# A two-block model on one core: the recurrence's first unit placed in the last input tile, and the key search of the expert stage spread differently

## The chip, the cores and the metric

One core of a Trainium2 chip runs the whole program in one launch. The metric is the device time of one execution in microseconds (us), the median of the runs taken. In the text TensorE is PE, VectorE is DVE, ScalarE is ACT, GpSimd is POOL and SyncE is SP, as in the profile's rows.

## The reference

256 tokens of width 2048 go through three layers, all in float32:

```python
def even_layer(x, ...):            # layer 1
    proj = rmsnorm(x, ln) @ w_in   # 2048 -> A: q, k, v, gate; B: q, f, i, gate
    ya = sliding_window_attention(...) * silu(ag)
    logf = logaddexp(log(max(lb, 1e-30)), log1p(-lb) + log_sigmoid(bf))
    ob = hgrn2_chunkwise(silu(bq), logf, -expm1(logf), bi)   # gated recurrence, 8 heads of 128
    yb = rmsnorm(ob, gn) * silu(bg)
    return x + concat([ya, yb]) @ w_out
def odd_layer(x, ...):             # layer 2: stick-breaking attention, 16 heads
    return x + (oc * silu(cg)) @ w_out
# layer 3: SSD and forgetting attention side by side, w_out, and then an expert layer
def peer(h, wq, k1, k2, u, v):
    q = (t @ wq).reshape(T, 8, 2, 128)
    v1, i1 = top_k(q[:, :, 0] . k1, 16);  v2, i2 = top_k(q[:, :, 1] . k2, 16)
    sc, pos = top_k(v1[..., :, None] + v2[..., None, :], 16)   # 16 of 256 pairs
    idx = 128 * i1 + i2 at pos;  g = softmax(sc)
    act = gelu(sum(u[idx] * t));  return sum(g * act * v[idx])  # 128 rows of u and of v per token
# and a last rmsnorm
```

The expert layer gathers 256 x 128 rows of 8 KB from `u` and as many from `v`.

## The kernel before, in words

**Projections.** Seven matrix products (even_in, even_out, odd_in, odd_out, two_in, two_out, peer_q) run in 57 tiles of 512 output columns. SP loads a tile's weights in four quarters into RAW. Each tile is split in eight subs: ScalarE rounds a sub of the weights to WH (`split`, L613), VectorE writes what the rounding left to WL (L1110), TensorE multiplies (HH, HL: the high and low part of the activations) with both (L1741). WH and WL hold four subs, so ScalarE can be at most four subs ahead of TensorE. Sub `s` of tile `t` is called place `8t + s`; every engine has a function `beside(place)` that puts work of other stages in front of a sub. The order of each engine's queue is thus written out by hand. A tile's result is taken out of its PSUM banks by `leave`, at sub 4 of the next tile or at the end of a phase. For a `silu` tile VectorE scales the result to BIG, and ScalarE applies silu to it (L565).

**The even layer.** Tiles 0 to 12 are even_in, 13 to 16 even_out. The gates of the recurrence are ready from place 91 on. TensorE turns the first log decays at place `B_TURN` = 101, ScalarE copies them to LFT at place 103. When even_in is over and its last tile has left, the recurrence runs over 16 units (8 heads x 2 halves of the tokens): `log_decays` (PE, ACT), `decays_low` (DVE), `level_sums` (PE, L2033 on), `decays` (ACT: Exp, L908), `query` (DVE, L1535), the key product (POOL, L472) `products` (PE), `masked` (DVE, L1547 on), `values` (PE), then per head a square sum and a norm (`normed`), and `y_high`, `y_low` put the result into HH and HL. The attention's eight outputs lie in BIG 3 and 4 and go to HH and HL in one operation each (`y_high_eight`, `y_low_eight`), before unit 1 overwrites them. Then tile 13 begins: ScalarE, VectorE and TensorE in turn.

**The expert stage.** Tiles 53 to 56 are peer_q. The key scores of a query tile are multiplied beside the next tile, the last ones behind tile 56. The key search of the first 128 tokens is cut in 4 pairs of heads with 8 steps each (`top_part`: steps 0 to 3 take the top 16 of 128, 4 and 5 the top 16 of 256 pairs, 6 and 7 the indices). It starts at place 439, one step a place: 17 steps fit. Then VectorE does 7 more, computes the normed tokens TT (L1696), and enters the loop over 256 picks (128 for each half of the tokens): one dot of 128x2048 with a gathered U row (L1701), the last 8 steps beside the first 8 dots, a small product every 4 picks for the coefficients; ScalarE then makes diagonals (L1036), and TensorE multiplies them with V rows. POOL issues all gathers (L533 and L542): U row n waits for dot n - 6 (six buffers), V row n - 8 follows it, and waits for TensorE's row n - 14. UROW lies on RAW and WL, so the first issue waits for the last split of tile 56, and the fifth for its last matmul. The second half's search goes beside picks 12 to 105, its step every third.

## Time and profile before

| what | value |
|---|---|
| median of 3 runs | 2936.0 us (2935.48 to 2937.61) |
| profiled execution | 2937.92 us, span 2936.2 us |
| granted TensorE clock, mean | 0.976 |
| busy in the span | PE 2467.8 us, DVE 1629.0, ACT 948.7, POOL 698.7 |
| DMA | 779.65 MB, of it 537.15 MB by POOL's queue (the gathered rows) |

Times in rows count from the span's start. A timeline row has start, duration, engine, line, operation, and in brackets how long the engine stood idle before it and what released it. A clock of 1.00 is 2.4 GHz, 0.50 is 1.2 GHz. The busy time of TensorE is modelled from pipelined matmuls, so it is no measure of use.

### The profile page before, as it was taken

The numbers are of one execution on the slowest core, as the hardware profiler recorded it, in microseconds if no ns is written. First come the engines' busy times: TensorE is split into PE (matmuls) and PEld (weight loads), VectorE is DVE, ScalarE is ACT, GpSimd is POOL, SyncE is SP. The second block draws the span as 40 slices with busy tenths as digits, with TensorE's granted clock in tenths as the row PEclk, the third lists the DMA queues.
The fourth block names the chain that finished last, engine by engine and source line by source line (L and its number), as shares of the span: only waits on it lengthen the run. The fifth ranks groups of instructions, "written<-read, shape, count | busy, mean of one in ns | idle before, by whom it ended". The sixth has DMA issues, their size and how long they took to land.

```text
span 2936.2 us, 30854 instructions
## 1 busy us (share of the span) xinstructions
PE 2467.8 (84%) x12244; PEld 1757.5 (60%) x12244; DVE 1629.0 (55%) x2253; ACT 948.7 (32%) x1548; POOL 698.7 (24%) x751
## 2 busy tenths in 40 slices
PE   7999888999999899999899287777777777777776
PEld 6997777899889789888689132222222322222222
DVE  4757495544455554456457966656555445444444
ACT  4557454533676444444554010000010001000001
POOL 5003151000000000540000243333333333333331
PEclk9999999999999999999899699999999999999999
DMA  5643304555444446333354799999999999999997
GB/s 190 212 147 129 129 1 144 172 186 179 153 157 158 158 135 215 129 115 116 101 191 139 315 406 421 421 422 421 422 421 422 421 422 422 421 422 422 421 422 319
DMA packets 200415, 779.65 MB, mean 266 GB/s; under 512 B 16564, under 2 KB 20880, under 8 KB 134096
## 3 DMA queue, kind: packets, MB, share of 16 engines
q0 software_dynamic: 74400, 537.15, 44.2%
q1 hardware_dynamic: 125872, 240.53, 24.7%
q8 instruction: 97, 1.59, 0.2%
q14 instruction: 46, 0.38, 0.0%
HBM read 775.54 MB, written 2.10 MB: 265 GB/s over the span
## 4 chain that ended last, share of the span: by engine, by line
DMA 34%; PE 26%; DVE 5%; issue 1%; ACT 1%; POOL 0%; DVEq 0%; ACTq 0%; POOLq 0%
DMA VROW<-in_peer_v_dram,WORK 34%; PE bank L1741 25%; DMA UROW<-in_peer_u_dram,WORK 1%; DVE WL L1110 1%; DVE BIG L1701 1%; DVE WORK L1406 0%; DVE BIG L1407 0%; DVE WORK L1409 0%; DVE WORK L1408 0%; PE bank L1800 0%; DVE WORK L1405 0%; ACT WH L613 0%; DVE BIG L1416 0%; DVE WORK L1418 0%; DVE BIG L1414 0%
## 5 line engine op out<-in xcount | busy, mean ns | idle before, releaser
L1741 PE MATMUL bank<-VROW,WORK 128*128 128x512 f32 x2024 | 928.5, 604 | 366.6 <-DMA VROW<-in_peer_v_dram,WORK 299.7
L1741 PEld LDWEIGHTS bank<-VROW,WORK 128*128 128x128 f32 x2024 | 368.4, 191 | 926.1 <-issue 744.6
L1701 DVE CUSTOM_DVE_ANT_0 BIG<-UROW,bank 128x2048 f32<-128x2048 f32 x256 | 585.5, 2288 | 562.6 <-DMA UROW<-in_peer_u_dram,WORK 548.0
L1110 DVE TENSOR_TENSOR WL<-RAW,WH 128x1024 fp32r<-128x1024 f32 (+2 forms) x456 | 543.0, 1200 | 528.7 <-ACT WH L613 527.3
L1741 PE MATMUL bank<-HH,WH 128*128 128x256 f32 x2128 | 609.1, 286 | 8.4 <-issue 4.8
L613 ACT ACTIVATE WH<-RAW 128x1024 fp32r<-128x1024 f32 (+2 forms) x456 | 464.2, 1034 | 445.1 <-PE bank L1741 444.7
L1741 PE MATMUL bank<-HL,WH 128*128 128x256 f32 x2128 | 603.3, 284 | 0.0
L1741 PE MATMUL bank<-HH,WL 128*128 128x256 f32 x2128 | 603.2, 283 | 0.0
L1741 PEld LDWEIGHTS bank<-HH,WH 128*128 128x128 f32 x2128 | 407.7, 192 | 15.9 <-issue 14.0
L1741 PEld LDWEIGHTS bank<-HL,WH 128*128 128x128 f32 x2128 | 407.8, 192 | 0.1
L1741 PEld LDWEIGHTS bank<-HH,WL 128*128 128x128 f32 x2128 | 407.7, 192 | 0.0
L542 POOL DMA_INDIRECT VROW<-in_peer_v_dram,WORK x256 | 241.7, 944 | 686.7 <-PE bank L1741 668.0
L533 POOL DMA_INDIRECT UROW<-in_peer_u_dram,WORK x256 | 243.7, 952 | 315.4 <-DVE WL L1110 195.1
L1741 PE MATMUL bank<-WH,HH 128*128 128x512 f32 (+1 forms) x736 | 291.4, 396 | 29.2 <-DVE WL L1110 29.2
L1045 ACT ACTIVATE WORK<-WORK 128x4 f32<-128x4 f32 x64 | 13.1, 205 | 920.1 <-DVE WORK L1701 920.1
L1741 PE MATMUL bank<-WH,HL 128*128 128x512 f32 (+1 forms) x736 | 287.1, 390 | 0.0
L1741 PE MATMUL bank<-WL,HH 128*128 128x512 f32 (+1 forms) x736 | 286.8, 390 | 0.0
L500 POOL TENSOR_SCALAR WORK<-GT,SM 128x128 f32<-128x128 f32 x16 | 19.5, 1219 | 713.9 <-DVE SM L1496 674.4
L1741 PEld LDWEIGHTS bank<-WH,HH 128*128 128x128 f32 x736 | 140.7, 191 | 60.4 <-issue 32.4
L1741 PEld LDWEIGHTS bank<-WL,HH 128*128 128x128 f32 x736 | 140.5, 191 | 28.8
L1741 PEld LDWEIGHTS bank<-WH,HL 128*128 128x128 f32 x736 | 140.8, 191 | 27.1
L1036 ACT ACTIVATE WORK<-ID,WORK 128x128 f32<-128x128 f32 x253 | 87.6, 390 | 211.9 <-PE bank L1741 206.2
(325 smaller groups left out, 1729.7 us busy)
## 6 DMA issues: line engine op xcount, KB each, us to landing
RAW<-in_w_in_odd_dram SPq DMA_DIRECT2D x64, 1024.0 KB, 5.1
RAW<-in_w_in_even_dram SPq DMA_DIRECT2D x48, 1024.0 KB, 5.0
RAW<-in_w_in_dram SPq DMA_DIRECT2D x44, 1024.0 KB, 4.9
RAW<-in_w_out_even_dram SPq DMA_DIRECT2D x16, 1024.0 KB, 5.0
RAW<-in_w_out_odd_dram SPq DMA_DIRECT2D x16, 1024.0 KB, 5.0
RAW<-in_w_out_dram SPq DMA_DIRECT2D x16, 1024.0 KB, 5.3
RAW<-in_peer_wq_dram SPq DMA_DIRECT2D x16, 1024.0 KB, 5.2
UROW<-in_peer_u_dram,WORK POOLq DMA_INDIRECT x256, 27.0
```

Source lines behind the costliest of these rows:

```text
L500: pool.tensor_scalar(g[:, 0:P], GT[:, :], lf[:, 0, h:h + 1], None, ALU.mult)
L533: pool.indirect_dma_start(UROW[:, n % ROWS_EACH, :], None, a["peer_u_2"], bass.IndirectOffsetOnAxis(ap=PICK[:, m, pick:pick + 1], axis=0))\
L542: pool.indirect_dma_start(VROW[:, v % ROWS_EACH, :], None, a["peer_v_2"], bass.IndirectOffsetOnAxis(ap=PICK[:, m, pick:pick + 1], axis=0))\
L613: act.activation(WH[:, sl:sl + 2, 0:w], raw[:, k0:k0 + 2, 0:w], ACT.Copy)\
L1036: act.activation(DIAG[:, k % 4, :], ID[:, :], ACT.Copy, scale=COEF[:, n:n + 1])\
L1045: act.activation(GELU[:, cols], DOT[:, cols], ACT.Gelu).then_inc(s["p_gelu"], 1)
L1110: dve.tensor_tensor(WL[:, sl:sl + 2, 0:w], raw[:, k0:k0 + 2, 0:w], WH[:, sl:sl + 2, 0:w].bitcast(F32), ALU.subtract).then_inc(s["wl_done"], 1)
L1701: dve.tensor_tensor_reduce(out=JUNK[:, n % 2, :], in0=UROW[:, b, :], in1=TT, op0=ALU.mult, op1=ALU.add, scale=1.0, scalar=0.0, accum_out=D ...
L1741: return pe.matmul(dst, lhsT, rhs, start=start, stop=stop, skip_group_check=True)
```

## The change

Two seams are changed.

In the even layer the transposes of the first two units' log decays move to places 95 and 98, their copies and low parts to 96 to 100, and `level_sums(0)` to place 101, in banks 2 and 3. `decays(0)`, `query(0)` and `products(0)` come before the last tile leaves; that tile's silu comes behind `decays(1)`. The attention's outputs go to HH and HL in two halves. LFL1 moves to another place in SBUF (onto RDIAG), so that unit 1's low part no longer overwrites them. Four subs of tile 13 are rounded and split within the recurrence, at iterations 6, 8, 10 and 12, and left out in the tile itself.

In the expert stage only pair 0 is searched inside tiles 54 to 56, one step every second place. Pairs 1 to 3 go beside picks 4 to 27, gates are made per pair, and the second half's search beside picks 29 to 91, a step every second. U rows 0 to 3 wait only for the splits whose RAW quarter they overwrite. The dots begin when half of the scores are out.

```diff
-TOP_AT, TOP_EVERY = 12, 3
+TOP_AT, TOP_EVERY = 29, 2
+TOP_INSIDE = TOP_STEPS
-B_TURN = 101
+B_TURN = 95
+B_LOW, B_TURN_1, B_LOW_1, B_LEVELS = 97, 98, 100, 101
...
# POOL
+                if u == 1:
+                    pool.wait_ge(s["y_l"], 8)
...
-                    if n == 0:
-                        pool.wait_ge(s["wl_done"], 8 * N_TILES)
+                    if n < 4:
+                        pool.wait_ge(s["wl_done"], 8 * (N_TILES - 1) + 2 * (n + 1))
...
# ScalarE
+                    if t == OUT_TILE and sub < 4:
+                        continue
...
+            def split_ahead(sub):
+                t = OUT_TILE
+                if sub % 2 == 0:
+                    act.wait_ge(s[f"w_full{sub // 2}"], 16 * (t + 1))
+                act.wait_ge(s["ws_used"], 8 * t + (sub - 3))
+                raw = RAW[:, sub // 2, :].rearrange("p (k n) -> p k n", k=4)
+                k0 = 2 * (sub % 2)
+                act.activation(WH[:, 2 * sub:2 * sub + 2, :], raw[:, k0:k0 + 2, :], ACT.Copy).then_inc(s["wh_done"], 1)
...
+            def y_high_four(kt, tile):
+                act.wait_ge(s["y_ready"], 8)
+                act.wait_ge(s["ws_used"], 8 * OUT_TILE)
+                act.activation(HH[:, kt:kt + 4, :], tile.rearrange("p (b t) -> p b t", t=T), ACT.Copy)\
+                    .then_inc(s["y_h"], 4)
...
-                if place == B_TURN + 2:
+                if place == B_TURN + 1:
                     log_decays(0)
+                if place == B_TURN_1 + 1:
+                    log_decays(1)
...
-                    act.wait_ge(s["y_l"], 8)
+                    act.wait_ge(s["y_l"], 4)
...
-            log_decays(1)
             decays(0)
-            y_high_eight(0, 0, BIG[:, 3:5, :])
+            y_high_four(0, BIG[:, 3, :])
+            y_high_four(4, BIG[:, 4, :])
...
+                if i == 0:
+                    leave(*pending.pop())
+                if i in (6, 8, 10, 12):
+                    split_ahead((i - 6) // 2)
...
+                if q in (3, 5, 7):
+                    gate_exp(0, (q - 1) // 2, 1)
...
# VectorE
+                if place == B_LOW:
+                    decays_low(0)
+                if place == B_LOW_1:
+                    decays_low(1)
-                step = step_at(place, TOP_FIRST, 1, TOP_STEPS * 4)
+                step = step_at(place, TOP_FIRST, 2, TOP_INSIDE)
...
-            decays_low(0)
-            y_low_eight(0, 0, BIG[:, 3:5, :])
-            decays_low(1)
             query(0)
+            leave(*pending.pop())
+            y_low_four(0, BIG[:, 3, :])
+            y_low_four(4, BIG[:, 4, :])
+            masked(0)
...
+                if i in (6, 8, 10, 12):
+                    split_ahead((i - 6) // 2)
...
-            inside = 8 * (Q_TILE + 4) - TOP_FIRST
-            for step in range(inside, 3 * TOP_STEPS):
-                top_part(0, step // TOP_STEPS, step % TOP_STEPS)
             dve.wait_ge(s["ln_in"], 16)
-            dve.wait_ge(s["q_s"], 8)
+            dve.wait_ge(s["q_s"], 4)
...
+                if n == 2:
+                    dve.wait_ge(s["q_s"], 8)
...
-                if n < TOP_STEPS:
-                    top_part(0, 3, n)
-                if n == TOP_STEPS:
-                    gates(0)
+                step = step_at(n, BATCH, 1, 3 * TOP_STEPS)
+                if step is not None:
+                    top_part(0, 1 + step // TOP_STEPS, step % TOP_STEPS)
+                if n == 4:
+                    gates(0, 0, 1)
+                i = step_at(n, 16, 10, 3)
+                if i is not None:
+                    gates(0, 1 + i, 1)
...
# TensorE
+                if place == B_TURN_1:
+                    log_decays(1)
+                if place == B_LEVELS:
+                    pe.wait_ge(s["tile_free"], OUT_TILE - 1)
+                    level_sums(0)
...
-            log_decays(1)
-            level_sums(0)
+            products(0)
+            pe.wait_ge(s["t_scaled"], sum(r["n"] for r in RUNS if r["phase"] == "even_in" and r["kind"] == "silu"))
```

## Rows read from the trace of the kernel before

**Rows 1.** Page, section 2: 40 slices of 73.4 us, what DMA moved.

```profile
GB/s 190 212 147 129 129 1 144 172 186 179 153 157 158 158 135 215 129 115 116 101 191 139 315 406 421 421 422 421 422 421 422 421 422 422 421 422 422 421 422 319
```

**Rows 2.** Page, section 4: the chain that ended last, shares by engine.

```profile
DMA 34%; PE 26%; DVE 5%; issue 1%; ACT 1%; POOL 0%; DVEq 0%; ACTq 0%; POOLq 0%
```

**Rows 3.** Windows: length, busy us (count) by engine, PEclk, DMA share, GB/s.

```profile
1605.00:1620.00 15.00, 14.72 (x123) 14.52 (x122) 14.24 (x35) 4.33 (x5) 0.00 (x0) 1.00 0.00 1
1620.00:1640.00 20.00, 7.02 (x57) 6.60 (x56) 18.62 (x60) 2.46 (x4) 6.11 (x6) 0.79 0.78 297
1620.00:1700.00 80.00, 25.14 (x95) 14.64 (x95) 76.36 (x172) 7.65 (x18) 27.92 (x29) 0.66 0.86 336
1750.00:2850.00 1100.00, 808.01 (x1758) 318.59 (x1759) 575.17 (x717) 92.22 (x291) 414.97 (x440) 0.99 1.01 422
```

**Rows 4.** Timeline of POOL, gathers of the expert stage.

```profile
1622.69 1.09 POOL L533 DMA_INDIRECT UROW<-in_peer_u_dram,WORK  x1 [195.15 <-DVE WL L1110]
...
1687.90 0.94 POOL L542 DMA_INDIRECT VROW<-in_peer_v_dram,WORK  x1 [6.26 <-PE bank L1741]
```

**Rows 5.** Timeline of DVE, from tile 56 to the first dots.

```profile
1585.94 1.23 DVE L1110 TENSOR_TENSOR WL<-RAW,WH 128x1024 fp32r<-128x1024 f32 x1
1589.57 1.22 DVE L1110 TENSOR_TENSOR WL<-RAW,WH 128x1024 fp32r<-128x1024 f32 x1
...
1620.58 1.23 DVE L1110 TENSOR_TENSOR WL<-RAW,WH 128x1024 fp32r<-128x1024 f32 x1
...
1639.03 2.36 DVE L1696 SCALAR_TENSOR_TENSOR bank<-XR,SM,BIG 128x2048 f32<-128x2048 f32 x1
...
1678.13 2.29 DVE L1701 CUSTOM_DVE_ANT_0 BIG<-UROW,bank 128x2048 f32<-128x2048 f32 x1
```

**Rows 6.** Timeline of ACT, roundings and score evictions of tile 56.

```profile
1602.53 1.06 ACT L613 ACTIVATE WH<-RAW 128x1024 fp32r<-128x1024 f32 x1 [0.91 <-PE bank L1741]
...
1612.88 1.06 ACT L613 ACTIVATE WH<-RAW 128x1024 fp32r<-128x1024 f32 x1 [1.76 <-PE bank L1741]
...
1628.32 0.69 ACT L801 ACTIVATE BIG<-bank,SM 128x512 f32<-128x512 f32 x1 [0.21 <-PE bank L1741]
```

**Rows 7.** Timeline of DVE, last eviction of even_in, mask of unit 1.

```profile
355.30 1.29 DVE L1081 TENSOR_TENSOR BIG<-bank,RS 128x512 f32<-128x512 f32 x2 [6.22 <-PE bank L1741]
...
375.48 0.68 DVE L1547 TENSOR_TENSOR WORK<-bank,BIG 128x512 f32<-128x512 f32 x1
```

**Rows 8.** Timeline of ACT, places 96 on and the first decays.

```profile
321.23 1.06 ACT L613 ACTIVATE WH<-RAW 128x1024 fp32r<-128x1024 f32 x1 [2.49 <-PE bank L1741]
...
358.39 1.28 ACT L908 ACT_TABLE_LOAD   x1
359.69 0.60 ACT L908 ACTIVATE WORK<-bank 128x512 f32<-128x512 f32 x1
```

**Rows 9.** Timeline of PE, the last attention values, at place 96.

```profile
331.01 0.86 PE L1741 MATMUL bank<-BIG 128*64 128x256 f32 x4
```

**Rows 10.** Windows inside the recurrence and at its end.

```profile
430.00:440.00 10.00, 8.24 (x62) 7.17 (x60) 9.78 (x14) 6.29 (x13) 5.87 (x3) 1.00 0.00 0
450.00:455.00 5.00, 1.23 (x7) 0.64 (x6) 1.34 (x3) 3.93 (x7) 0.00 (x0) 0.88 0.00 0
```

**Rows 11.** Timelines of DVE and POOL, one y_low and one key product.

```profile
435.05 2.30 DVE L1163 TENSOR_TENSOR HL<-YB,HH 128x256 fp32r<-128x256 f32 x1
...
434.93 2.13 POOL L472 TENSOR_TENSOR WORK<-WORK,BIG 128x896 f32<-128x896 f32 x1 [0.35 <-ACT WORK L908]
```

**Rows 12.** Timeline of PE, end of the recurrence, first matmul of tile 13.

```profile
452.84 0.70 PE L1741 MATMUL bank<-BIG,ONES 128*128 128x256 f32 x2 [2.31 <-ACT BIG L915]
...
460.08 0.77 PE L1741 MATMUL bank<-WH,HH 128*128 128x512 f32 x1 [6.54 <-DVE WL L1110]
```

**Rows 13.** Timeline of ACT, fifth rounding of tile 13.

```profile
465.02 1.06 ACT L613 ACTIVATE WH<-RAW 128x1024 fp32r<-128x1024 f32 x1 [3.50 <-PE bank L1741]
```

**Rows 14.** Page, section 5: the V row matmuls.

```profile
L1741 PE MATMUL bank<-VROW,WORK 128*128 128x512 f32 x2024 | 928.5, 604 | 366.6 <-DMA VROW<-in_peer_v_dram,WORK 299.7
```

More of the change, by code:

```diff
@@ L123 @@
 ODD_TILE = last_tile("even_out") + 1
+OUT_TILE = first_tile("even_out")
 C_FIRST = 8 * ODD_TILE + 70
@@ L907, in decays @@
                 for b in range(2):
-                    ins = act.activation(B_EX[u % 2][:, 512 * b:512 * (b + 1)], bank[b][:, :], ACT.Exp)
+                    ins = act.activation(B_EX[u % 2][:, 512 * b:512 * (b + 1)], bank[b if u else 2 + b][:, :], ACT.Exp)
                 ins.then_inc(s["b_ex"], 1)
@@ L1008, in _, with gate_exp @@
             scores_out(3)
-            def gate_exp(m):
-                act.wait_ge(s["tk_e"], 4 * (m + 1))
-                act.activation(GATE[:, m * PICKS:(m + 1) * PICKS], GATE[:, m * PICKS:(m + 1) * PICKS], ACT.Exp)\
-                    .then_inc(s["tk_g"], 1)
+            def gate_exp(m, i, pairs):
+                act.wait_ge(s["tk_e"], 4 * m + i + pairs)
+                cols = GATE[:, m * PICKS + 32 * i:m * PICKS + 32 * (i + pairs)]
+                act.activation(cols, cols, ACT.Exp).then_inc(s["tk_g"], pairs)
             def square(b):
@@ L1105, in split @@
                             leave(*pending.pop())
+                    if t == OUT_TILE and sub < 4:
+                        continue
                     dve.wait_ge(s["wh_done"], 8 * t + sub + 1)
@@ L1113, in split, with split_ahead @@
                     pending.append((r, i, parity, t))
+            def split_ahead(sub):
+                dve.wait_ge(s["wh_done"], 8 * OUT_TILE + sub + 1)
+                raw = RAW[:, sub // 2, :].rearrange("p (k n) -> p k n", k=4)
+                k0 = 2 * (sub % 2)
+                dve.tensor_tensor(WL[:, 2 * sub:2 * sub + 2, :], raw[:, k0:k0 + 2, :],
+                                  WH[:, 2 * sub:2 * sub + 2, :].bitcast(F32), ALU.subtract).then_inc(s["wl_done"], 1)
             def phase(name):
                 over_tiles(dve, name, split)
-                if not name.endswith("out"):
+                if not name.endswith("out") and name != "even_in":
                     leave(*pending.pop())
@@ L1164, in y_low, with y_low_four @@
                                   ALU.subtract).then_inc(s["y_l"], 1)
+            def y_low_four(kt, tile):
+                dve.wait_ge(s["y_h"], kt + 4)
+                dve.tensor_tensor(HL[:, kt:kt + 4, :], tile.rearrange("p (b t) -> p b t", t=T),
+                                  HH[:, kt:kt + 4, :].bitcast(F32), ALU.subtract).then_inc(s["y_l"], 4)
             def y_low_eight(c, kt, tiles):
@@ L1459, in beside @@
                         dve.wait_ge(s["tk_iota"], 1)
-                    top_part(0, step // TOP_STEPS, step % TOP_STEPS)
+                    top_part(0, 0, step)
                 for n in range(1, 4):
@@ L1652, in _, with gates @@
             phase("peer_q")
[L1653 to L1659 removed]
+            def gates(m, i, pairs):
+                dve.wait_ge(s["tk_g"], 4 * m + i + pairs)
+                g3 = GATE[:, m * PICKS + 32 * i:m * PICKS + 32 * (i + pairs)].rearrange("p (h k) -> p h k", k=16)
+                gs = gsum[:, 0:2 * pairs]
+                link(dve.tensor_reduce(gs, g3, AX.X, ALU.add))
+                link(dve.reciprocal(gs, gs))
+                link(dve.tensor_tensor(g3, g3, gs.unsqueeze(2).broadcast_to([P, 2 * pairs, 16]), ALU.mult))
             def coefficients(q):
@@ L1710, in _ @@
                 if n == GATES_AT:
-                    gates(1)
-                if n == TOP_STEPS:
-                    coefficients(0)
-                if n > TOP_STEPS and n % BATCH == 1:
+                    gates(1, 0, 4)
+                if n > BATCH and n % BATCH == 1:
                     coefficients(n // BATCH - 1)
@@ L1805, in phase @@
                 over_tiles(pe, name, tile)
-                if not name.endswith("out"):
+                if not name.endswith("out") and name != "even_in":
                     pe.wait_ge(s["tile_free"], last_tile(name) + 1)
@@ L1933, in log_decays, with level_sums @@
                     .then_inc(s["b_lt"], 1)
+            def level_sums(u):
+                m = u % 2
+                if u == 0:
+                    pe.wait_ge(s["b_ms"], 4)
+                pe.wait_ge(s["b_ll"], u + 1)
+                if u >= 1:
+                    pe.wait_ge(s["b_ex"], u)
+                if m == 0:
+                    ends = MSR[:, 512:1024]
+                else:
+                    ends = MSR[:, 512:1536 - 256].rearrange("p (a b) -> p a b", b=256)[:, 0:3:2, :]
+                first = bank[0] if u else bank[2]
+                mm(first, LFT[:, m, :], MSR[:, 0:512], True, False)
+                mm(first, LFL[m], MSR[:, 0:512], False, True)
+                dst = bank[1].rearrange("p (a b) -> p a b", b=256) if m else bank[1] if u else bank[3]
+                mm(dst, LFT[:, m, :], ends, True, False)
+                mm(dst, LFL[m], ends, False, True).then_inc(s["b_es"], 1)
             keys = KEYS.rearrange("p (f d) -> p f d", f=16)
```

55 lines of the change are left out of this document (16 added, 39 removed).

## The prediction

> **What bounds the kernel now.** I read the slices of the page first [rows 1]: up to some 1600 us DMA moves 1 to 215 GB/s, then from slice 25 on 421 to 422 in all but the last. The chain that ended last says the same [rows 2]: projections on TensorE, then expert rows by DMA. So each half has its own currency: before the expert stage a microsecond counts if TensorE's order of work gets shorter; in it, if DMA starts earlier or idles less. The change touches one seam in each half, and the windows and timelines around the two seams give the rest.
>
> **Seam B, the start of the expert stage.** From 1605 to 1620 us DMA moves 1 GB/s [rows 3]. The first U row is issued at 1622.69 [rows 4], right behind the last split of the input tile (1620.58, 1.23 us) [rows 5]. From 1620 to 1700 us the queues move 336 GB/s, in the steady stretch 422 [rows 3]: 80 x 336 / 422 = 63.7 us of work in 80, so 16.3 us lost. Why is in the timeline of VectorE [rows 5]: after the last split VectorE does the rest of pair 2 and the expansion TT (1639.03), so the first dot starts at its end, 1641.4. Six row buffers fill, then wait for a dot at every step of the key search that is woven in. The ninth dot starts at 1678.13; eight picks with eight steps take 36.7 us, 4.59 each.
>
> One pick is two row sets of 1.049 MB, 2.485 us each at 422 GB/s, 4.97 together. New order, in the times of the profile of before:
> - VectorE puts 8 steps on places 439 to 453 instead of 17 on 439 to 455. The split of place 452 waits for ScalarE's rounding (1602.53 + 1.06) [rows 6], and so ends near 1604.8. Step 7 takes 3.63 - 1.15 = 2.5 us (the distance of two splits less one split) [rows 5]: the indices of pair 0 are ready at 1607.4. U rows 0 to 2 follow at about 1607.5 to 1610. Row 3 follows the last split, which no longer queues behind steps: rounding at 1612.88 [rows 6] + 1.06 + 1.23 = 1615.2.
> - Those four rows (9.9 us of transfer) run where DMA idles today. TT then runs from 1615.2 to 1617.6, dots 0 and 1 to 1622.3. Dot 2 waits for the last scores, which are evicted from 1628.32 on [rows 6]: 1628.2 to 1630.6.
> - Row 4 waits for the last matmul of the tile, about 1624.2, and is issued near 1625.0 (before, the issue followed the split's end by 0.9 us). Before, the first issue at 1622.69 was worth full rate from 1625.9: 1640 less 20 x 297 / 422 = 14.1 us for what had moved [rows 3]. That is 3.2 us after the issue; I take 2.9, as TensorE ends the tile 0.3 us sooner without the late splits. Full rate from 1627.9.
> - Rows 4 to 7 keep DMA busy until 1637.8, and the reload of LNF 2.5 us more. Row 8 is free to go at 1630.7, so there is no gap. From dot 4 on VectorE needs 4.59 us for a pick with a step, and I put 0.14 on it for coefficient products and the smaller gates (three or four instructions of 0.2 to 0.3 us in eight picks): 4.73 against 4.97 of DMA. It stays ahead by little, and the backlog at dot 8 is some 15 us.
> - V rows no longer start with ScalarE and TensorE far behind. Before, V row 6 is issued at 1687.90, after 6.26 us of waiting for TensorE [rows 4]. Now diagonal 0 is made after dot 7 (1649), and v_used 1 comes near 1655.5, before POOL needs it with dot 8's row.
>
> Sum: the old stream is worth a start at 1620 + 16.3 = 1636.3 for 512 row sets; the new one 1627.9 for 508, that is 1627.9 - 9.9 = 1618.0. Gain 18.3 us. Bounds: 13 if VectorE loses 5 us in the first 24 picks, 20 if the ramp is shorter. The search of the second 128 tokens only moves its 32 steps within the loop (29 to 91 instead of 12 to 105); a dot is 2.3 of the 4.59, a step the other 2.3, so a pair of picks there costs 6.9 us under 9.9: nothing. The waits on wl_done and the smaller exponentials cost nothing for the same reason.
>
> **Seam A, the recurrence.** Removed in front: before, TensorE ends the even input tile at 355.1 (VectorE's eviction at 355.30 is released by it) [rows 7], ScalarE does silu and an Exp table load and makes the first decays at 359.69 [rows 8], and the mask of unit 1 starts at 375.48 [rows 7]. After, the first unit's decays, query and key products are made inside the tile. What this adds there:
> - ScalarE at place 96 now waits for a transpose that TensorE issues at place 95. Before, ScalarE rounds place 96 at 321.23 [rows 8] while TensorE is at place 92; place 96 begins at 331.0 [rows 9]. So ScalarE's queue stands 7 us, and its four places of lead shrink to one; rounding 1.06 and split 1.23 just fit into a place of 2.82 (1.06 busy and 1.76 waiting at 1612.88) [rows 6]. At place 99 the same once more: it waits for place 98, which begins at 331.2 + 0.86 + 2 x 2.82 = 337.7. Behind it stands the eviction of tile 11 at place 100: VectorE ends split 99 at 340.6, the low part and the eviction at 342.2, silu at 343.3, rounding 344.3, split 345.6. TensorE wants it at 337.7 + 0.2 + 2 x 2.82 = 343.6: a stall of 2.0 us. With the two transposes and four matmuls of level_sums (0.93 us, work moved and not new) the tile ends at 357.9, not 355.1. Bounds: 0.9 to 5 us.
> - After it, with the durations of before (a half of HH 1.0 us, a half of HL 1.2, a mask 2.1): products(0) at once, HH and HL until 362.0, mask 0 until 364.1, decays of unit 1 at 361.3, silu with its table load until 364.8, Exp load and decays of unit 2 until 367.6. Query 2 and the key product of unit 2 then start together, and mask 1 starts between 368.9 and 370.5. Against 375.48 this is 5.0 to 6.6 us earlier; I take 6.0.
>
> Added in the loop: four roundings on ScalarE (1.06 each, hidden: it is busy 6.29 of 10 us there) and four splits on VectorE. VectorE is busy 9.78 of 10 us there [rows 10], so nothing hides them: 4 x 1.2 = 4.8 us. From both sides: 0, if each falls into the wait that y_low has now, and 9.6, if each also meets a GpSimd operation. The row for this: the y_low of 128x256 takes 2.30 us at 435.05 and ends at 437.35, as the key product on GpSimd (434.93 to 437.06) does [rows 11]. A split in front of it takes over that wait and adds its own 1.2 behind, so I stay at 4.8. By the Trainium skill (SBUF — State Buffer, Who interferes with whom), a VectorE instruction with two SBUF inputs and a GpSimd instruction that reads SBUF lock one another out for a whole instruction, by issue order. The trace agrees with 2.30 us against 1.23 for a tile four times as wide. By that rule a split that issues first could hold back the next 0.6 us GpSimd product as well; with 0.6 x 4 the price would be 7.2.
>
> Removed behind: TensorE's last work of the loop is at 452.84 and ends at 453.5; its next matmul waits for the split until 460.08 [rows 12]. The four first splits are done by then, so TensorE goes on at 453.5. Before, the first eighth of the tile ends at 465.0 (ScalarE's rounding at 465.02 is released by it) [rows 13]. After, it ends at 453.5 + 2.7 = 456.2 at full clock. The later eighths are rounded from 457.7 on, and TensorE wants the fifth at 464.4: no new wait. Gain 8.7 us. The clock is a risk: it is 0.88 over 450 to 455 [rows 10], the full level until about 453.8 and then 1.2 GHz. Were it to fall with TensorE at work, up to 2 us are lost.
>
> By the Trainium skill (ScalarE: Activation LUTs, What ACT_TABLE_LOAD costs) a change of table set costs about 2.66 us with its drain. The trace does not agree: a load of 1.28 at 358.39 is followed by the exponential at 359.69 [rows 8]. By the page's price the two loads around the moved silu would take 2.8 us more from seam A.
>
> Seam A: 6.0 - 4.8 + 8.7 = 9.9 us. Everything between the seams is paced by TensorE and moves as a whole.
>
> **Total.** 18.3 + 9.9 = 28.2 us. The profiled execution has a span of 2936.2 and took 2937.9; it becomes 2908.0 and 2909.7. The median, 2936.0, is 1.9 us below the profiled run: 2907.8.
>
> **Rivals.**
> - B only: seam A gives nothing. The places at 96 to 100 cost 5 instead of 2.8, each loop split meets a lock (9.6), and the clock falls at the tail (2): 9.9 - 2.2 - 4.8 - 2 = 0.9. Then 2936.0 - 19.2 = 2916.8. For it: VectorE is full; against: all three have to come.
> - VectorE becomes the bound of the first 24 picks: a pick with a step needs 5.4 instead of 4.73, 0.43 over DMA's 4.97, so 24 x 0.43 = 10 us, and 2918. Against: the 4.59 are measured with DMA at full rate.
> - Slower: TensorE stays at 1.2 GHz in the expert stage. Today it wakes on six V rows that lie ready. After, it gets four diagonals at a time and may stand between. The mean clock over 1620 to 1700 is 0.66 [rows 3]. A V row takes 928.5 / 253 = 3.67 us at full clock [rows 14], 7.3 at half, 2.4 more than DMA needs for a pick. From 12 such picks on (28 / 2.4) the gain is gone; with 40, 2936 - 28 + 96 = 3004. Against: the steady stretch keeps 0.99 with TensorE busy 808 of 1100 us, so idle 1.3 in every pick [rows 3].
> - The U rows before the tile's end don't overlap (the indices come too late): 9.9 us less, 2917.7.
>
> **Chances.** Forecast 0.72, B only 0.12, VectorE bound 0.05, early rows lost 0.05, slower 0.03; 0.03 for a gain that is larger, as no stall at place 100 and free splits give 2900. 0.2% of this kernel, 5.9 us, is about what a measurement can tell from no change. Range 2898 to 2920: down by the 6.8 of the cheap ends of seam A and 2 of the ramp, up to the cases that lose one seam. Faster 0.95, same 0.02, slower 0.03.
>
> **What would show it.** Three or four U issues before the last matmul of the last query tile and DMA busy there; the first dot near 1617 less the shift of seam A; no window under 400 GB/s from 10 us after; TensorE's first output-tile matmul within 1 us of the last square sum; y_low or split of 2.3 us or more in the loop; a gap of some 2 us at place 100. Wrong would be: dots 5 to 27 spaced over 4.97 on average, PEclk at 0.5 behind dot 20, or a loop longer by over 7 us.

## The result and the profile after

The median went from 2936.8 us (four runs, 2935.5 to 2937.6) to 2916.6 us (four runs, 2916.3 to 2917.2), a ratio of 0.9931 with a 95% interval of 0.9916 to 0.9945. In another group of runs, on other executions of both kernels, it came out at 2916.8 and 0.9932 [0.9918, 0.9945]. The forecast was 2907.8, range 2898 to 2920. So the sign and the range held, and 8.1 us of the gain are missing: 20.1 instead of 28.2.

The two seams are read one by one. First the DMA rate in the 40 slices of the page after, the row that answers to [rows 1]:

```profile
GB/s 191 210 152 130 130 15 130 173 188 179 155 155 163 159 135 206 128 116 131 89 186 160 368 421 421 421 421 421 422 422 421 413 422 422 422 421 422 421 422 313
```

The steady rate starts in the 24th slice, before in the 25th, and the 23rd has 368 instead of 315. One slice of 72.9 us has 413 for 421; before has no such slice. The windows that answer to [rows 3] (same columns):

```profile
1605.00:1620.00 15.00, 14.88 (x125) 14.68 (x123) 9.31 (x7) 2.20 (x3) 4.53 (x3) 1.00 0.76 277
1620.00:1640.00 20.00, 2.02 (x16) 1.86 (x16) 16.14 (x36) 3.99 (x7) 12.12 (x13) 0.67 0.91 362
1620.00:1700.00 80.00, 49.42 (x111) 21.44 (x112) 73.67 (x166) 10.90 (x25) 36.77 (x38) 0.83 0.99 407
1750.00:2850.00 1100.00, 812.71 (x1757) 319.56 (x1755) 584.36 (x751) 92.24 (x291) 416.39 (x440) 0.99 1.01 421
```

Where DMA moved 1 GB/s it moves 277, the 80 us behind it have 407 instead of 336, and the steady stretch is as before. The timelines of GpSimd (gathers) and VectorE (dots) after, which answer to [rows 4, 5]:

```profile
1603.14 1.10 POOL L539 DMA_INDIRECT UROW<-in_peer_u_dram,WORK  x1 [180.19 <-DVE WORK L1505]
...
1610.99 2.80 POOL L539 DMA_INDIRECT UROW<-in_peer_u_dram,WORK  x1 [3.96 <-DVE WL L1149]
1620.16 0.94 POOL L539 DMA_INDIRECT UROW<-in_peer_u_dram,WORK  x1 [6.36 <-PE bank L1804]
```
```profile
1613.03 2.29 DVE L1762 CUSTOM_DVE_ANT_0 BIG<-UROW,bank 128x2048 f32<-128x2048 f32 x1
...
1623.31 2.29 DVE L1762 CUSTOM_DVE_ANT_0 BIG<-UROW,bank 128x2048 f32<-128x2048 f32 x1 [5.54 <-PE bank L1804]
...
1636.59 2.29 DVE L1762 CUSTOM_DVE_ANT_0 BIG<-UROW,bank 128x2048 f32<-128x2048 f32 x1
...
1640.63 2.29 DVE L1762 CUSTOM_DVE_ANT_0 BIG<-UROW,bank 128x2048 f32<-128x2048 f32 x1
...
1644.68 2.29 DVE L1762 CUSTOM_DVE_ANT_0 BIG<-UROW,bank 128x2048 f32<-128x2048 f32 x1
```

The first dot is at 1613.03 instead of 1641.4. These three dots with a short search step between them are 4.05 us apart (1636.59, 1640.63, 1644.68). The steps are not alike: over dots 5 to 27 the mean distance is 4.71 us and the longest 6.32. The mean is under the 4.97 that DMA needs for a pick.

Seam A lost its lead on the way. VectorE after: the last eviction of the input tile and the mask of unit 1, which answer to [rows 7].

```profile
357.50 1.29 DVE L1117 TENSOR_TENSOR BIG<-bank,RS 128x512 f32<-128x512 f32 x2 [6.35 <-PE bank L1804]
...
368.83 0.69 DVE L1604 TENSOR_TENSOR WORK<-bank,BIG 128x512 f32<-128x512 f32 x1
```

The mask is 6.65 us earlier than in before, and the first norm 6.6. (A norm's time is here the start of its last VectorE instruction, the subtraction of 128x256.) Then come four pairs of steps with a split. One of them, VectorE and under it GpSimd after (answers to [rows 11]):

```profile
404.20 1.92 DVE L1617 TENSOR_TENSOR YB<-YB,BIG 128x256 f32<-128x256 f32 x1
...
409.29 3.10 DVE L1159 TENSOR_TENSOR WL<-RAW,WH 128x1024 fp32r<-128x1024 f32 x1
```
```profile
403.75 2.09 POOL L478 TENSOR_TENSOR BIG<-BIG 128x896 f32<-128x896 f32 x1 [3.51 <-ACT BIG L936]
...
408.84 2.47 POOL L478 TENSOR_TENSOR WORK<-WORK,BIG 128x896 f32<-128x896 f32 x1 [3.00 <-ACT WORK L936]
```

The split starts 0.45 us behind a key product of GpSimd and takes 3.10 us instead of the 1.23 that it takes elsewhere. In the same pair a two-input subtraction of 128x256, 0.42 us elsewhere, starts 0.45 us behind the other key product and takes 1.92. A pair took 10.54 us before; with a split the distances of the norms are 11.66, 12.48, 12.35 and 12.37, together 6.7 us more. TensorE at the end of the recurrence after, which answers to [rows 12]:

```profile
445.68 3.48 PE L1804 MATMUL bank<-BIG 128*128 128x128 f32 x16 [2.15 <-DVE AMB L1605]
...
455.13 0.70 PE L1804 MATMUL bank<-BIG,ONES 128*128 128x256 f32 x2 [2.49 <-ACT BIG L943]
455.48 0.58 PE L1804 MATMUL bank<-WH,HH 128*128 128x512 f32 x1
```

The next projection does start right behind the last square sum, without a wait, but at 455.48 and not at 453.5, and with TensorE's clock at the lower level twice on the way. Windows of after (columns as in [rows 10]):

```profile
445.00:450.00 5.00, 4.32 (x22) 4.30 (x23) 2.37 (x5) 0.39 (x2) 0.00 (x0) 0.66 0.01 3
450.00:455.00 5.00, 2.26 (x18) 1.87 (x17) 2.24 (x5) 3.95 (x6) 0.00 (x0) 1.00 0.00 0
455.00:460.00 5.00, 4.87 (x14) 3.91 (x15) 1.18 (x3) 3.93 (x6) 0.00 (x0) 0.66 0.00 0
```

ScalarE's fifth rounding of the tile, which answers to [rows 13]:

```profile
460.26 1.06 ACT L622 ACTIVATE WH<-RAW 128x1024 fp32r<-128x1024 f32 x1 [0.24 <-PE bank L1804]
```

460.26 instead of 465.02: 4.8 us of seam A are left.

### The profile page after: what moved, and what is told of

Same layout as the page of the kernel before. It is cut to its first block, busy times and chain, and to the rows that moved or that the text cites. A ratio compares the mean times of both kernels' runs of the same rounds, so it can differ in the third digit from the quotient of the medians.

```text
span 2915.5 us, 30891 instructions
## 1 busy us (share of the span) xinstructions
PE 2481.9 (85%) x12244; PEld 1761.7 (60%) x12244; DVE 1630.7 (56%) x2263; ACT 957.8 (33%) x1560; POOL 702.0 (24%) x751
## 4 chain that ended last, share of the span: by engine, by line
DMA 35%; PE 27%; DVE 3%; issue 1%; ACT 1%; POOL 0%; DVEq 0%; ACTq 0%; POOLq 0%
DMA VROW<-in_peer_v_dram,WORK 34%; PE bank L1804 27%; DVE BIG L1762 1%; DMA UROW<-in_peer_u_dram,WORK 1%; PE bank L1863 0%; DVE WL L1149 0%; PE bank L1906 0%; ACT WH L622 0%; DVE WORK L1459 0%; DVE BIG L1460 0%; DVE WORK L1462 0%; DVE WORK L1461 0%; DVE BIG L1705 0%; DVE XR L1732 0%; DVE HL L1646 0%
## 5 line engine op out<-in xcount | busy, mean ns | idle before, releaser
L1804 PE MATMUL bank<-VROW,WORK 128*128 128x512 f32 x2024 | 941.8, 611 | 337.7 <-DMA VROW<-in_peer_v_dram,WORK 298.4
```

Of the source, the lines that this page charges most:

```text
L1804: return pe.matmul(dst, lhsT, rhs, start=start, stop=stop, skip_group_check=True)
```

## The experiments

One yardstick beside the time is used for all of them, from the traces: the stretch from TensorE's matmul at the start of place 96 (331.01 before, [rows 9]; 330.52 after) to ScalarE's sixth rounding of tile 13 (467.71 before, 462.95 after). It holds seam A and nothing else. "Late splits" are the four first splits of tile 13.

| kernel | median us | ratio to before | stretch |
|---|---|---|---|
| before | 2936.2 to 2938.4 (by group) | 1 | 136.7 |
| after | 2916.6, again 2916.8 | 0.9931, 0.9932 | 132.4, 132.4 |
| seam A alone | 2931.6 | 0.9985 [0.9976, 0.9994] | 131.1 |
| seam B alone | 2920.4 | 0.9946 [0.9933, 0.9960] | 134.9 |
| no split ahead | 2915.6 | 0.9928 [0.9915, 0.9942] | 131.3 |
| roundings only | 2915.4 | 0.9929 [0.9916, 0.9943] | 130.0 |
| one split ahead | 2912.9 | 0.9915 [0.9902, 0.9929] | 130.4 |
| reductions | 2915.3 | 0.9923 [0.9908, 0.9938] | 130.3 |
| copies | 2921.9 | 0.9950 [0.9935, 0.9965] | 137.8 |
| front moved | 2915.8 | 0.9925 [0.9912, 0.9939] | 130.5 |
| tail splits | 2907.5 | 0.9898 [0.9883, 0.9913] | 123.6 |
| both | 2905.3 | 0.9889 [0.9874, 0.9904] | 121.5 |
| rows late | 2919.4 | 0.9941 [0.9928, 0.9955] | 131.6 |

Differences of 1 to 2 us between medians lie within these intervals. Nor does the stretch decide them by itself, since it is read from one execution each: four traces whose code is the same in it (after twice, seam A alone, rows late) have 131.1 to 132.4, and before and seam B alone have 136.7 and 134.9. Where a difference of that size matters, single rows have to carry it.

**The yardstick.** The changed kernel unchanged, in the last group but one.

> The changed kernel as it is, a second time, as the yardstick of this group of runs: 2916.6 (2915.5 to 2917.5), a ratio of 0.993 to the kernel before.

Measured 2916.8. Its trace repeats the loop: norms at 381.28, 391.78, 403.44, 415.91, 428.27, 440.62.

**Seam A alone and seam B alone.** Each takes back the hunks of the other. Of the first:

```diff
-TOP_AT, TOP_EVERY = 29, 2
+TOP_AT, TOP_EVERY = 12, 3
-                    if n < 4:
-                        pool.wait_ge(s["wl_done"], 8 * (N_TILES - 1) + 2 * (n + 1))
+                    if n == 0:
+                        pool.wait_ge(s["wl_done"], 8 * N_TILES)
```

Of the second:

```diff
-B_TURN = 95
-B_LOW, B_TURN_1, B_LOW_1, B_LEVELS = 97, 98, 100, 101
+B_TURN = 101
-                if i in (6, 8, 10, 12):
-                    split_ahead((i - 6) // 2)
```

> Seam A alone: the first unit's front inside the last input tile and the splits ahead in the loop; the expert stage as before. Theory (the two seams are independent, and the trace after shows the first tile of the next projection 4.8 us earlier): 4.8 us below before, 2932.0 (2930.5 to 2933.5). Rival (the seams interact, and part of the expert stage's gain hangs on seam A): under 3 us below before. The prediction on record had 9.9 us for it, 2926.9.

> Seam B alone: the thinner key search joined into the last projection tile of the expert stage; the recurrence as before. Theory: what is left of 20.1 us after seam A's 4.8, so 15 to 18 us below before, 2919 to 2922 (17.9 at the first picks, some 2 us lost later among the picks). The prediction on record had 18.3 us for it, 2918.5. Rival (seam B fell short and seam A gave its 9.9): 10 us below before, 2926.5.

Measured against before of the same group: 4.6 and 15.8 us less, together 20.4 of 20.1. The seams add, as far as the intervals can tell. What is missing of the forecast is 5.3 us of seam A (4.6 for 9.9) and 2.5 of seam B (15.8 for 18.3), each with an uncertainty of 2.6 to 4 us by the intervals. The traces divide it the same way: in the profiled execution of seam B alone the last dot is 17.6 us earlier than before's, and 1.9 of that arises ahead of the sixth rounding of tile 13, where this kernel's code is before's; 15.7 are left for seam B.

**No split ahead, and roundings only.** The first puts all of the late splits back into the tile; the second does so for VectorE's subtractions alone and leaves ScalarE's four roundings in the loop:

```diff
-                    if t == OUT_TILE and sub < 4:
-                        continue
-                if i in (6, 8, 10, 12):
-                    split_ahead((i - 6) // 2)
```

> The kernel after, with no split of the next projection's weights ahead: ScalarE's roundings and VectorE's subtractions are back in the first tile behind the loop. Theory (the four splits cost the loop 6.7 us and its tail 2.3, and save only the wait ahead of the first matmul): the pairs of steps take 10.54 us again, the loop and its tail end about 9 us sooner, and TensorE waits about 6.5 us for the first split behind it and 3 to 5 us for the second, as before; time 0.5 to 3 us below after, 2914 to 2916. Rival (the splits ahead are worth what they were meant to be, 8.7 us behind the loop against 4.8 in it): 3 to 5 us above after, 2920 to 2922.

> The kernel after with ScalarE's four roundings ahead in the loop and VectorE's four subtractions back in the tile. Theory (it is VectorE's 128x1024 subtraction, 3.10 us beside GpSimd's key product, that stretches four pairs of steps): pairs at 10.54 us again, loop 6.7 us shorter, the first matmul behind it waits for a subtraction of about 1.3 to 2.5 us; time 3 to 7 us below after, 2910 to 2914. Rival (the roundings on ScalarE delay the evictions of the steps): pairs of the four units stay at 11.7 to 12.5 us and the time is at or above after.

The first thus undoes everything that was done for tile 13 and keeps the moved front. Both have pairs of 10.54 us again; so ScalarE's roundings cost the loop nothing, and VectorE's splits cost all of it. But the times, 2915.6 and 2915.4, are hardly under after: the first as the theory had it, the second above its range of 2910 to 2914. The loop with roundings ends early (last norm of a full pair at 435.34 for 441.40), and then TensorE stands. TensorE in the kernel with roundings only:

```profile
446.88 1.22 PE L1799 MATMUL bank<-BIG,ONES 128*128 128x256 f32 x2 [2.31 <-ACT BIG L943]
453.50 0.76 PE L1799 MATMUL bank<-WH,HH 128*128 128x512 f32 x1 [5.40 <-DVE WL L1146]
```

I had expected a wait of 1.3 to 2.5 us. It is 5.4, since VectorE takes its instructions in order and the first split stands behind the norm and low part of the last unit, which end at 452.2. Of the 6.7 us that the pairs gained, 2.4 are left in the stretch (130.0 for 132.4). So the splits ahead are worth having; their place is wrong.

**Tail splits.** The same work, put behind the last key products of GpSimd:

```diff
 # ScalarE
-                if i in (6, 8, 10, 12):
-                    split_ahead((i - 6) // 2)
+                if i == 15:
+                    for sub in range(4):
+                        split_ahead(sub)
 # VectorE
-                if i in (6, 8, 10, 12):
-                    split_ahead((i - 6) // 2)
+                if i in (15, 17):
+                    split_ahead(2 + (i - 15) // 2)
...
+                if i == 14:
+                    split_ahead(0)
+                    split_ahead(1)
```

> The kernel after with the same four splits ahead put into the gaps of the last units (after the last GpSimd key product) instead of into four full pairs of steps. Theory (a split beside GpSimd's product stretches the pair, and without splits ahead VectorE's in-order queue puts the first split behind the last unit's norm, 5.4 us of TensorE's waiting in the run with roundings alone): pairs at 10.54 us, first matmul of the next projection right behind the last square sum, near 448 us instead of 455.5; 6 to 8 us below after, 2908.5 to 2910.5. Rival (the four splits cost their VectorE time wherever they stand): the tail is 3 to 5 us longer, 2 to 4 us below after, 2912.5 to 2914.5.

Measured 2907.5, 9.2 us under after, more than the theory had. VectorE and then TensorE in this kernel:

```profile
438.55 2.35 DVE L1160 TENSOR_TENSOR WL<-RAW,WH 128x1024 fp32r<-128x1024 f32 x2
...
442.74 1.22 DVE L1160 TENSOR_TENSOR WL<-RAW,WH 128x1024 fp32r<-128x1024 f32 x1
```
```profile
445.68 1.22 PE L1808 MATMUL bank<-BIG,ONES 128*128 128x256 f32 x2 [1.42 <-ACT BIG L943]
446.34 0.99 PE L1808 MATMUL bank<-WH,HH 128*128 128x512 f32 x1
```

All four splits take their bare 1.2 us in gaps of VectorE, behind the end of GpSimd's last key product (437.75), the pairs stay at 10.54, and the projection starts at 446.34 instead of 455.48. This is the 8.9 us of the stretch (123.6 for 132.4).

**Front moved.** The copies of the first unit's transposes and their low halves go to later places, so that ScalarE doesn't stand in front of its roundings:

```diff
-B_LOW, B_TURN_1, B_LOW_1, B_LEVELS = 97, 98, 100, 101
+B_LOW, B_TURN_1, B_LOW_1, B_LEVELS = 98, 99, 102, 101
-                if place == B_TURN + 1:
+                if place == B_TURN + 3:
                     log_decays(0)
-                if place == B_TURN_1 + 1:
+                if place == B_TURN_1 + 3:
                     log_decays(1)
```

> The kernel after with the first unit's front begun one place earlier in the last input tile and its copies and low halves moved off the queue spot where they held TensorE. Theory (the front's lead is what the tile's places allow, and TensorE's idle time around place 100 is a stall of the queues): the first mask some 2 us earlier, and nothing else changed behind it; 1 to 2.5 us below after, 2914 to 2915.5. Rival (the tile's evictions on VectorE and ScalarE set the front's pace): within 0.5 us of after, 2916.6.

(The first words are wrong: the front begins at place 95 as in after; the copies, the low halves and the second unit's transpose moved, the last to place 99.) Measured 2915.8, between the theory's range and the rival's, so the time decides nothing. The trace shows 1.9 us in the stretch (130.5 for 132.4), and all of it is in the front: from place 96 to the first norm it takes 49.6 us, and 51.5 to 52.3 in the four traces with after's code. ScalarE after, then ScalarE in this kernel, at the same two copies:

```profile
327.76 0.28 ACT L820 ACTIVATE LFT<-bank 128x128 fp32r<-128x128 f32 x1 [9.61 <-PE bank L1995]
...
337.47 0.28 ACT L820 ACTIVATE LFT<-bank 128x128 fp32r<-128x128 f32 x1 [6.21 <-PE bank L1995]
```
```profile
327.99 0.28 ACT L820 ACTIVATE LFT<-bank 128x128 fp32r<-128x128 f32 x1 [2.54 <-PE bank L1995]
...
340.58 0.28 ACT L820 ACTIVATE LFT<-bank 128x128 fp32r<-128x128 f32 x1 [1.93 <-PE bank L1995]
```

ScalarE's waits of 9.61 and 6.21 us have shrunk to 2.54 and 1.93, and TensorE's stall at place 100 is gone (1.52 us idle ahead of 344.70 after, none here).

**Both.** The last two edits together.

> The last two edits together. Theory (they act on different stretches of one chain and add): 8 to 10 us below after, 2906.5 to 2908.5, below both kernels. Rival (TensorE's clock or the tail absorbs the lead): no better than the better of the two by itself, 2909 to 2910.5.

Measured 2905.3, a ratio of 0.9889 [0.9874, 0.9904], 33.2 us under before in its own group and 11.4 under after. Stretch: 121.5, the sum of the two gains (8.9 + 1.9 = 10.8, measured 10.9). This is the fastest version of this study.

**Reductions and copies.** What is it in a split that hurts? Both kernels have the late splits in the tile, roundings and subtractions, so the kernel to compare them with is the one with no split ahead. At the four places of the loop stands instead a reduction of 128x1024, or a copy of 128x1024:

```diff
                 if i in (6, 8, 10, 12):
-                    split_ahead((i - 6) // 2)
+                    dve.tensor_reduce(SM[:, 146:147], raw, AX.X, ALU.add)
```

```diff
                 if i in (6, 8, 10, 12):
-                    split_ahead((i - 6) // 2)
+                    dve.tensor_copy(WL[:, 2 * sub:2 * sub + 2, :], raw[:, k0:k0 + 2, :])
```

In both, `raw` is the piece of RAW that the split would read.

> The kernel after with its splits back in the tile, and at the four places of the loop, in place of each split, a VectorE reduction over 128x1024 with one tensor input, whose result is not used. Theory (what stretches a pair is that a VectorE instruction with two tensor inputs from on-chip memory and GpSimd's product shut each other out, 3.10 us beside it against 1.23 alone): the reduction takes about 1.1 us beside the product, the subtraction behind the norm keeps 0.42 us, and each pair gains 0 to 1.1 us, 0 to 4.4 in all. Rival (VectorE's queue is full and any 1.2 us instruction costs as much as the split): the four pairs grow by 1.1 to 1.9 us each, 6.7 in all, as in after.

> As the kernel with reductions in place of the splits ahead, but with a VectorE copy of 128x1024 from on-chip memory to the split's own place, rounded as the split rounds: one tensor input, and the split's whole output. Theory (two tensor inputs are what meets GpSimd's product): the copy takes 1.1 to 1.3 us beside the product, pairs stay at 10.54 us, 2914.5 to 2916. Rival (the writing of 1024 columns is what meets it): the copy takes 2 to 3 us and the pairs grow by 1 to 2 us each, 2919 to 2922.

The reductions cost nothing: 1.21 us each, right beside a key product, pairs of 10.54. The loop isn't full in the sense that I had meant; VectorE's busy time of 9.78 in 10 us [rows 10] contains the y_low's 2.30 us of waiting [rows 11], and this falls to 1.18 behind the reduction. VectorE with reductions, and then with copies:

```profile
408.31 1.21 DVE L1627 TENSOR_REDUCE SM<-RAW 128x1 f32<-128x1024 f32 x1
409.44 1.18 DVE L1202 TENSOR_TENSOR HL<-YB,HH 128x256 fp32r<-128x256 f32 x1
```
```profile
397.30 2.56 DVE L1628 CAST WL<-RAW 128x1024 fp32r<-128x1024 f32 x1
...
404.69 2.91 DVE L1584 TENSOR_TENSOR BIG<-BIG 128x1024 f32<-128x1024 f32 x1
...
411.06 0.68 DVE L1628 CAST WL<-RAW 128x1024 fp32r<-128x1024 f32 x1
```

The copies refute my narrower theory: one tensor input is not what saves the reduction. Alone a copy takes 0.68 us (411.06), little more than half of the reduction; issued 0.12 us behind a key product it takes 2.56. The pairs grow to 11.12, 11.88, 11.87 and 11.88, and the time to 2921.9 (rival: 2919 to 2922). By the Trainium skill (SBUF — State Buffer, Who interferes with whom), a reduction never takes the ports that VectorE shares with GpSimd, while a copy can do so in its doubled mode, and "Issue order, not op shape, decides who blocks"; the trace agrees on all three, with 1.21, with 0.68 against 2.56, and with what follows.

In the last three pairs the copy itself cost 0.68 us and met nothing, and yet they are 1.3 us longer. The rows show why. At 404.69 VectorE's query product (L1584) comes 0.47 us behind GpSimd's big key product (404.22) and takes 2.91 us. With reductions it is issued at 404.65, 0.04 us ahead of GpSimd (404.69): VectorE keeps its 1.23 us, and GpSimd pays. GpSimd with copies, then VectorE and GpSimd with reductions:

```profile
404.22 2.29 POOL L478 TENSOR_TENSOR BIG<-BIG 128x896 f32<-128x896 f32 x1 [4.04 <-ACT BIG L933]
```
```profile
404.65 1.23 DVE L1584 TENSOR_TENSOR BIG<-BIG 128x1024 f32<-128x1024 f32 x1
...
404.69 3.15 POOL L478 TENSOR_TENSOR BIG<-BIG 128x896 f32<-128x896 f32 x1 [4.30 <-ACT BIG L933]
```

**One split ahead.** Does such a turn of the order persist?

```diff
-                    if t == OUT_TILE and sub < 4:
+                    if t == OUT_TILE and sub == 0:
...
-                if i in (6, 8, 10, 12):
-                    split_ahead((i - 6) // 2)
+                if i == 6:
+                    split_ahead(0)
```

> The kernel after with ScalarE's four roundings ahead and a single VectorE split ahead, in the first of the four pairs; the other three are back in the tile. Theory (the copies run showed pairs of 11.88 us although a copy itself took only 0.68 us: once a pair is late, GpSimd's big key product starts before VectorE's query product instead of after it, VectorE waits for it, and the order stays so): the pair with the split grows by some 1.1 us and the following ones take 11.0 to 11.9 us without a split, 3 to 5 us more in the loop than with roundings alone; 1 to 4 us of it seen in the time, 2916.5 to 2919.5. Rival (each split pays for itself alone): one pair of 11.7 us, then 10.54 again; within 1 us of the run with roundings alone, 2914.5 to 2916.4.

Neither. The distances of the norms are 10.52, 11.66 (with the split), 11.23 (the pair behind it), 10.54, 10.54: the turned order of the big key product lasts for one pair, and then the old one is back. One split costs 1.12 + 0.69 = 1.81 us, which is the 1.81 and 1.83 of the third and fourth split in after. The median, 2912.9, is below both ranges; its five runs lie between 2910.7 and 2915.7, so no more is read from it.

**Rows late.** The first U rows wait for the last split of the tile, as in before:

```diff
-                    if n < 4:
-                        pool.wait_ge(s["wl_done"], 8 * (N_TILES - 1) + 2 * (n + 1))
+                    if n == 0:
+                        pool.wait_ge(s["wl_done"], 8 * N_TILES)
```

> The kernel after, but the first four groups of U rows wait for all eight splits of the last projection tile, as in the kernel before; the key search stays thinned and joined in. Theory (the early rows are what lets the first dots start at 1613 us, and the stream of rows runs at its full rate from then on): the first group is issued at about 1615 instead of 1603, 7 to 10 us above after, 2924 to 2927. Rival (the chain of the key search releases everything behind the first rows, so the early issue is hidden anyway): within 1 us of after, 2916.6.

Measured 2919.4, 2.6 us over after, and 3.4 if one counts that its stretch happens to be 0.8 us shorter. That is between the theory and the rival. The runs of the two kernels in this group don't overlap (2915.0 to 2918.2, and 2919.1 to 2920.8). Windows of this kernel:

```profile
1610.00:1615.00 5.00, 5.00 (x44) 5.00 (x43) 3.12 (x2) 0.00 (x0) 2.96 (x2) 1.00 0.13 20
1615.00:1620.00 5.00, 5.00 (x42) 4.81 (x41) 1.19 (x1) 0.00 (x0) 2.21 (x3) 1.00 0.91 351
1620.00:1640.00 20.00, 2.04 (x17) 1.86 (x16) 15.06 (x26) 4.07 (x7) 9.48 (x11) 0.65 1.01 419
```

By 1620 after has moved 15 x 277 GB/s = 4.16 MB and this kernel 1.86: 2.30 MB or 5.5 us ahead. By 1640 it has lost 20 x (419 - 362) = 1.14 MB or 2.7 us of that again. The four early sets have landed when the fifth is issued at 1620.16, so DMA stands until it runs; late rows are still in flight then.

## Why the forecast was right in sign and too large in size

**Seam B, the steps.** Seam A brings the last quarter of the projections 4.8 us forward (the second projection's first halves of HH: 557.18 before, 552.42 after), so 4.8 is taken from each forecast time. First gather 1607.5: 1602.7, measured 1603.14. Row 3 after 1615.2: 1610.4, measured 1610.99. First dot 1617.6: 1612.8, measured 1613.03. Dot 2 between 1628.2 and 1630.6: 1623.4 to 1625.8, measured 1623.31. Row 4 at 1625.0: 1620.2, measured 1620.16. All steps held within 0.6 us.

**Seam B, the sum.** Forecast 18.3. The dots of picks 28 to 40 are 22.3 to 22.7 us earlier than before's, some 17.7 without seam A's share; so the sum was nearly right up to there. Then the lead shrinks: 22.7 us up to pick 41, 21.7 from 43 on, 21.3 at 252, 20.3 in the last three dots, and 20.7 in the whole span. The kernel with seam B alone loses its microsecond at the same pick (19.7, then 18.7) and another in the last three; it measures 15.8. So some 2 us are lost among the picks, one near pick 42 and up to one at the end. The slice with 413 GB/s is not where it happens: it covers picks 128 to 142, and the lead is 21.5 before and behind it. In the repeat the same slice has 420, and its lead shrinks as much (23.5 to 21.6). What is different at pick 42 and in the last three was not tried and stays open.

**Rival "B only".** Its number, 2916.8, is nearly the measured 2916.6, and this is luck. It wanted nothing from seam A (0.9) and all 18.3 from seam B; seam A alone gives 4.6, seam B alone 15.8. Of its three prices the places at 96 to 100 cost 2.7 us and not 5, the splits 1.81 each and not 2.4, and only the fall of the clock came in. The rival "early rows lost" had 2917.7 and fits as well by its number and as little by its rows. And the range held because it reached up to the cases that lose a whole seam, not because each term was right.

**Rival "VectorE becomes the bound".** Out, and the forecast's price held: 4.71 us from dot to dot on average over dots 5 to 27, for 4.73. Single steps need 4.05 to 6.32; the rows in the buffers even that out.

**Rival "early rows lost".** Out: DMA moves 277 GB/s ahead of 1620. Its 9.9 us, for no overlap at all, were not tested, since the thinner search by itself ends the last split near 1611 instead of 1621.8 and even late rows are issued at 1611.74, within the tile. What the early issue adds to that is 2.6 to 3.4 us.

**Rival "TensorE stays at 1.2 GHz".** Out: 0.83 over 1620 to 1700 for 0.66, and 0.81 to 0.91 in each 20 us from 1640 on.

**Seam A, front: 6.0.** Right. 6.65 us at the mask, 6.1 by the stretch. The stall at place 100 was forecast as 2.0 and the tile's end as 2.8 later; measured 1.52 of waiting and 2.7 (24.3 and 27.0 us from place 96 to the eviction), and moving the copies gave 1.9.

**Seam A, loop: -4.8.** This is the first wrong size: 6.7 in the four pairs and 2.2 behind them (last full norm to last norm 15.55 before, 17.75 after). The step that failed is "a split in front of it takes over that wait and adds its own 1.2 behind". It does take over the wait (3.10 us). But I left out that the later phase turns the order of the two products, so that VectorE waits for the big key product too. This costs 0.69 per split more, which the row with one split shows by itself: 1.81 each, not 1.2. The prediction also had 7.2, by the rule of the Trainium skill that it names (SBUF — State Buffer, Who interferes with whom), and stayed with the nearer row. The lock by issue order is what the rows show, and 4 x 1.81 is 7.2; but that the sizes agree is partly luck. The small product that the prediction thought of is indeed held back (1.43 us behind a split, 0.63 without one), while the 0.69 come with the next big product, which now starts ahead of VectorE. From the first norm to the last the loop takes 77.1 us for 68.3: 8.9 longer, beyond the 7 that the prediction had named as a sign of being wrong.

**Seam A, tail and behind: +8.7.** The wait for the first split is gone as forecast (6.54 us, none after), and the stretch from the last norm to the sixth rounding is 7.1 us shorter (10.85, 3.80). The clock risk of 2 us came in, and twice. In the tail sixteen matmuls take 3.48 us for 2.02 behind a wait of 2.15 us for VectorE, at a granted clock of 0.66 over 445 to 450, so partly at 1.2 GHz. And the projection's first ten matmuls are 0.43 us apart, 0.23 later: its first eighth takes 4.8 us where the forecast had 2.7 at full clock. (Before, the first nine were 0.43 apart too; so this is a gain that didn't come, and not a loss.) In the kernel with seam A alone, whose code is the same here, the fall comes one group earlier (fourteen matmuls in 3.33 us, 1.80 elsewhere) and the tail is 1.6 us shorter. TensorE in that kernel:

```profile
440.90 3.33 PE L1796 MATMUL bank<-WORK 128*128 128x128 f32 x14 [1.21 <-DVE AMB L1600]
...
446.17 2.02 PE L1796 MATMUL bank<-BIG 128*128 128x128 f32 x16 [0.57 <-DVE AMB L1600]
```

In all: 6.1 - 6.7 - 2.2 + 7.1 = 4.3 us of the stretch, 4.8 with the drift of 0.5 between the two traces ahead of place 96; forecast 9.9. The rest is seam B's 2 us. The -2.2 in the tail has two parts. With seam A alone, and with rows late, where the fall comes earlier, the tail takes 16.1 us: 1.6 less than after's 17.75, which is what the late fall costs, and 0.6 more than before's 15.55. These 0.6 are near the 0.69 that the single split left behind it; that they are the same thing is an inference.

## What to carry to other kernels

Before an instruction is moved onto an engine that shares a resource with another, look not at how much that engine is busy but at what runs beside the new place: the same four splits cost 1.7 us each beside GpSimd's products and nothing in the tail, 40 us later. Ask also what a shift of half a microsecond does to the order of two instructions that start within 0.1 us of each other, since the loser pays the whole of the other's duration. And when a wait is taken away in front of an engine, read the queue in front of the next one: without VectorE's splits ahead the four pairs got 6.7 us shorter, and then TensorE waited 5.4 us for a split that stood behind other work in VectorE's queue.

## What was not expected of the hardware

The order of two such instructions differs between two kernels whose code is the same there. In the recurrence of before and of the kernel with seam B alone VectorE's query product and GpSimd's key product start within 0.6 us of each other. VectorE and GpSimd in before, then in the kernel with seam B alone:

```profile
372.66 2.90 DVE L1535 TENSOR_TENSOR WORK<-WORK,BIG 128x1024 f32<-128x1024 f32 x1
...
372.12 2.36 POOL L472 TENSOR_TENSOR WORK<-WORK,BIG 128x896 f32<-128x896 f32 x1
```
```profile
372.54 1.21 DVE L1540 TENSOR_TENSOR WORK<-WORK,BIG 128x1024 f32<-128x1024 f32 x1
...
372.53 3.18 POOL L473 TENSOR_TENSOR WORK<-WORK,BIG 128x896 f32<-128x896 f32 x1 [0.66 <-ACT WORK L909]
```

Where GpSimd started 0.5 us ahead, VectorE took 2.90 us; where both started within 0.01 us, VectorE took its 1.21 and GpSimd 3.18. The stretch is 1.8 us shorter there (134.9 for 136.7), 1.2 of it up to the first norm: in sum as much as the 1.81 that a split costs in the loop.

The rows also show what turned the order. TensorE in before, then with seam B alone, and the window 368 to 370 of each (columns as in [rows 3]):

```profile
367.45 2.22 PE L1741 MATMUL bank<-WORK 128*128 128x128 f32 x14
...
368.00:370.00 2.00, 2.00 (x17) 2.00 (x16) 1.20 (x2) 0.77 (x2) 1.15 (x1) 0.88 0.00 0
```
```profile
367.32 2.75 PE L1749 MATMUL bank<-WORK 128*128 128x128 f32 x14
...
368.00:370.00 2.00, 2.00 (x13) 2.00 (x13) 1.23 (x1) 0.65 (x2) 1.27 (x1) 0.64 0.00 0
```

With seam B alone TensorE stays at 1.2 GHz half a microsecond longer (granted 0.64 over these 2 us, 0.88 before). These matmuls end later, ScalarE's exponentials of the next decays start at 371.37 instead of 370.95, and GpSimd, which waits for them, starts 0.41 us later, while VectorE doesn't. Why the clock rose later there stays open.

A copy that alone is twice as fast as a reduction was the dearer of the two here: 6.3 us over the kernel with no split ahead (2921.9 for 2915.6, and 6.5 by the stretch), where the reductions were at its level (2915.3).
